# A two-sided recurrence on one core: half products and steps move only the 32 columns of a block that a level changes, and leave them packed in PSUM

## The reference, cut to what matters

```
def step(state, inp):
    r_t, w_t, k_t, v_t, kk_t, a_t = inp
    sa = jnp.einsum('bhvk,bhk->bhv', state, -kk_t)
    state = (state * w_t[:, :, None, :] + sa[..., None] * (kk_t * a_t)[:, :, None, :]
             + v_t[..., None] * k_t[:, :, None, :])
    return state, jnp.einsum('bhvk,bhk->bhv', state, r_t)
```

## Time and profile before

| | |
|---|---|
| median of 3 runs | 2564.86 us (2564.17 to 2568.09) |
| the profiled execution's own time | 2562.55 us |
| its span, first to last instruction | 2560.8 us |
| mean granted clock of PE | 0.994 of 2.4 GHz |
| PE, PEld, DVE, ACT, POOL busy | 2453.5, 2112.5, 1086.6, 475.1, 178.8 us |
| first and last half product (L3688) | 2061.2 and 2306.9 us |
| L3688, L3701 records | 1280; 1280 and 1024 |
| L3504, L3978 | 80 each |

### The profile page before, as it was taken

How to read it: one execution, slowest core, us unless ns; L and a number is a source line. 1 busy time by engine, 2 the same in 40 slices (tenths; PEclk the granted TensorE clock), 3 DMA queues, 4 the chain that set the end, 5 groups by cost and what they waited for, 6 DMA issues and landing times. The chain is left out here.

```text
span 2560.8 us, 80261 instructions
## 1 busy us (share of the span) xinstructions
PE 2453.5 (96%) x36137; PEld 2112.5 (82%) x36137; DVE 1086.6 (42%) x2659; ACT 475.1 (19%) x1059; POOL 178.8 (7%) x225
## 2 busy tenths in 40 slices
PE   7999999999999999999999999999999989989998
PEld 7898878789889989999999898777758767777775
DVE  4682554477321010110101102446764378866666
ACT  2111000211132323210000001410010445542000
POOL 0100000010022322210000000000000001110000
PEclk9999999999989999999999999999999999999999
DMA  7444553554589999999999999326564000020453
GB/s 234 154 148 139 175 164 131 171 179 149 202 306 407 408 407 408 407 408 407 407 407 407 407 406 329 116 90 200 197 209 161 3 7 8 7 71 26 166 177 117
DMA packets 289906, 571.11 MB, mean 223 GB/s; under 512 B 18190, under 2 KB 180244, under 8 KB 289764
## 3 DMA queue, kind: packets, MB, share of 16 engines
q1 hardware_dynamic: 289764, 569.10, 60.9%
HBM read 567.98 MB, written 5.28 MB: 224 GB/s over the span
## 5 line engine op out<-in xcount | busy, mean ns | idle before, releaser
L2669 PE MATMUL ps<-xg,ring 128*64 128x80 f32 x14336 | 508.6, 233 | 6.3 <-issue 4.7
L2669 PEld LDWEIGHTS ps<-xg,ring 128*64 128x64 f32 x14336 | 502.1, 138 | 10.9 <-issue 6.6
L2792 DVE TENSOR_TENSOR hidden<-acted,ps 128x320 f32<-128x320 f32 x64 | 28.5, 446 | 661.8 <-PE ps L2669 661.8
L2685 PE MATMUL ps<-hidden,expert_down 128*64 128x80 f32 x7168 | 257.3, 233 | 11.1 <-DMA expert_down<-in_moe_w_down_dram 5.3
L2685 PEld LDWEIGHTS ps<-hidden,expert_down 128*64 128x64 f32 x7168 | 251.4, 137 | 14.2 <-issue 9.8
L2734 ACT ACTIVATE ring<-second 128x1792 f32<-128x1792 f32 x60 | 101.9, 1699 | 213.4 <-PE ps L2669 139.8
L631 PE MATMUL ps<-xT,ring 128*128 128x256 f32 (+1 forms) x592 | 133.1, 384 | 3.1 <-DMA ring<-in_w_in_dram 3.1
L631 PEld LDWEIGHTS ps<-xT,ring 128*128 128x128 f32 (+1 forms) x592 | 107.0, 183 | 26.4 <-issue 3.5
L2726 POOL COPY ring<-second 128x1792 f32<-128x1792 f32 x60 | 100.9, 1681 | 309.4 <-PE ps L2669 181.1
L631 PE MATMUL ps<-ring,xT 128*128 128x256 f32 (+1 forms) x544 | 108.9, 361 | 2.2 <-PEq L1136 2.2
L631 PEld LDWEIGHTS ps<-ring,xT 128*128 128x128 f32 x544 | 96.0, 190 | 14.5 <-issue 3.0
(11 more groups left out here) (617 smaller groups left out, 3918.5 us busy)
## 6 DMA issues: line engine op xcount, KB each, us to landing
expert_down<-in_moe_w_down_dram SPq DMA_DIRECT2D x96, 1024.0 KB, 17.2
ring<-in_mlp_w_dram SPq DMA_DIRECT2D x64, 1024.0 KB, 5.3
ring<-in_moe_w_gate_dram SPq DMA_DIRECT2D x68, 896.0 KB, 16.0
ring<-in_moe_w_up_dram SPq DMA_DIRECT2D x68, 896.0 KB, 16.6
second<-in_moe_w_gate_dram SPq DMA_DIRECT2D x30, 1792.0 KB, 18.9
second<-in_moe_w_up_dram SPq DMA_DIRECT2D x30, 1792.0 KB, 18.8
ring<-in_w_xkv_dram SPq DMA_DIRECT2D x16, 1024.0 KB, 5.4
expert_down<-in_moe_w_down_dram SPq DMA_DIRECT2D x32, 512.0 KB, 16.5
```

What stands on the lines that cost most here:

```text
L2669: mm = pe.matmul(bank[b][o:o + HEAD, at, :], w[:, c, f * P + o:f * P + o + HEAD], xg[:, p * E_STEP + c, :], start=(p == 0 and c == 0 and a ...
L2685: mm = pe.matmul(yT[c // 4][o:o + HEAD, c % 4, :], w[:, j, c * P + o:c * P + o + HEAD], hidden[:, f, :], start=False, stop=False, skip_gro ...
L2792: dve.tensor_tensor(hidden[:, part, :], acted[:, part, :], src, ALU.mult).then_inc(hidden_ready, 1)
```

## The change

Half products and steps now move only the 32 columns that the level can change, and write them without gaps. `changing` picks them in the source. The half product writes 4 x 32 columns instead of 4 x 64, ACT copies those 128 columns and scatters them into Pb at their places, and the step writes its two kinds side by side into the last 128 columns of bank A(d) and the first 128 of B(d). DVE's predicated copy reads this packed stretch; it still moves 256 elements per partition (128 at level 5) into the same places of XX. Pb's other columns keep what is in them, which nothing reads into a result, so POOL fills both Pb with zeros at the start, and ACT waits for that once before the first pair. The weights keep 64 columns.

```
-        def both_kinds(d):
-
-            return ps[:, A(d):B(d) + 1, :].rearrange("p a b -> p (a b)")[:, 4 * HEAD:]
+        PART = HEAD // 2
+
+        def both_kinds(d, k):
+
+            packed = ps[:, A(d):B(d) + 1, :].rearrange("p a b -> p (a b)")[:, 12 * PART:20 * PART]
+            return packed.rearrange("p (r n m b) -> p r n m b", r=2, n=4, b=1 << k)
...
-            at = n * HEAD
+            at = n * PART
             if region(kind, d):
-                return ps[:, B(d), at:at + HEAD]
-            return ps[:, A(d), 4 * HEAD + at:4 * HEAD + at + HEAD]
+                return ps[:, B(d), at:at + PART]
+            return ps[:, A(d), 12 * PART + at:12 * PART + at + PART]
+
+        def changing(block, k, kind, d):
+
+            return block.rearrange("p (m z b) -> p m z b", z=2, b=1 << k)[:, :, region(kind, d), :]
...
+                pool.memset(Pb[0][:], 0.0)
+                pool.memset(Pb[1][:], 0.0).then_inc(self.cleared.sem, 1)
...
-                    act.activation(Pb[d][:].rearrange("p a b -> p (a b)"), ps[:, A(d), 0:4 * HEAD], ACT.Copy).then_inc(q["half_ready"].sem, 1)
+                    to = changing(Pb[d][:].rearrange("p a b -> p (a b)"), k, 0, d)
+                    act.activation(to, ps[:, A(d), 0:4 * PART].rearrange("p (m b) -> p m b", b=1 << k), ACT.Copy).then_inc(q["half_ready"].sem, 1)
...
+                act.wait_ge(self.cleared.sem, self.cleared.at(2))
...
-                            mm = pe.matmul(ps[other, A(d), n * HEAD:(n + 1) * HEAD], GM[d][h, n, 0, h], XX(i, d, 0, n)[h], start=True, stop=True)
+                            mm = pe.matmul(ps[other, A(d), n * PART:(n + 1) * PART], GM[d][h, n, 0, h], changing(XX(i, d, 0, n)[h], k, 0, d), start=True, stop=True)
...
-                                mm = pe.matmul(made(d, kind, n)[on], p if kind else xt, xt if kind else p, start=True, stop=True)
+                                mm = pe.matmul(made(d, kind, n)[on], p if kind else xt, changing(xt if kind else p, k, kind, d), start=True, stop=True)
...
-                    x, fresh, places = moved(XXs[d][i % 2][:], k), moved(both_kinds(d), k), places_of(k)
+                    x, fresh, places = moved(XXs[d][i % 2][:], k), both_kinds(d, k), places_of(k)
```

## The result

The changed kernel takes 2582.05 us (median of 6 runs, 2576.72 to 2585.77), the kernel before 2564.86 beside it (five runs): a ratio of 1.0059, 95% interval 1.0046 to 1.0071. It is slower, by 15 us by the ratio and 17 by the medians, and lies outside the range of the forecast (2553 to 2568). The profiled execution took 2579.67 us, 17.1 more than that of before; its span is 2577.9, the mean granted clock 0.980 (0.994 before).

The account below looks back on a forecast made before the run. No engine is full; PE's in-order chain waits for ACT's copy in four of ten slots, with DVE's slack limiting gains. Shorter copies and ends save 0.67 us a pair, 8 x 0.67 = 5.3: 2564.86 - 5.3 = 2559.5 us, range 2553 to 2568.

Parts of the forecast that it names:

- rival 3: PE's clock falls at levels 4 and 5; one dip in each pair gives 2569.2 us, two in some more; chance 0.16.
- A dip as long as the one from 1352.3 to 1355.7: Price of one clock fall at levels 4 and 5: it holds 1.4 slowed slots and costs 1.2 us.
- Decides from five dips on: Number of clock dips at which their 1.2 us each outweighs the 5.3 us gain (5.3 / 1.2 = 4.4).
- The main case: Shorter copy and ends save 0.67 us a pair, 5.3 in all: 2559.5 us, own range 2557.5 to 2562; chance 0.58.
- The pace of half products and steps: PE's records: the 64-wide weights set about 56 ns per record, so halving the moving columns changes nothing.
- rival 1: Weights don't bind PE; half products and steps each lose 0.22 us, DVE caps the gain: 2555.3 us; chance 0.12.
- ACT's copy: Copy of half products, 256 to 128 elements, saves 0.11 us in each of four slots at levels 4 and 5.
- The ends: The last record of a PE group ends 28 ns sooner, 0 as lower bound; alone worth 8 x 0.23 = 1.8 us.
- DVE's fit of 0.04 us: Last level-5 copy: DVE can start at 2208.50, PE asks for it at 2208.54, so it just fits.
- the cap that the prediction named: DVE has about as much slack as the change can give PE, which limits every gain.
- DVE's lead: From the first level-4 copy DVE runs 0.28 us ahead: 0.14 from its waiting there, 0.14 from earlier work.
- The level-1 copy: DVE's level-1 copy stays at 0.72 us; if the source in PSUM slows it, 0.3 us shorter, 1.5 in all.

Follow-up runs that it names:

- e1: The changed kernel plus one unused 128-column matmul before each step of levels 4 and 5; 2560.79 us, ratio 0.9977 to the kernel before.
- e5: The changed kernel plus the unused 128-column matmul before each step at level 4 alone; 2573.88 us, ratio 1.0029.
- e3: The changed kernel with steps of 64 columns again, not packed; half products and ACT's copy stay cut; 2563.75 us, ratio 0.9995.
- e8: e3 plus the unused matmul before each step at level 4; 2566.74 us, ratio 1.0007.
- e2: The kernel before with only ACT's copy cut to the changed columns, and the fills of Pb; 2564.19 us, ratio 0.9995.
- e4: The changed kernel with half products and ACT's copy of 64 columns again, only the steps cut; 2569.79 us, ratio 1.0013.
- e12: The changed kernel plus the unused 128-column matmul before each step at level 5 alone; 2577.82 us, ratio 1.0051.
- e7: The changed kernel with the next stage's weight loads begun after the last pair's first chunk is solved; 2572.35 us, ratio 1.0022.
- e6: The changed kernel plus 16 unused matmuls before each level-4 step, weights 32 or 64 wide by direction, to measure the pace; 2575.5 us in a single execution.
- e9: The kernel before with the next stage's weight loads begun after the last pair's first chunk is solved; 2563.95 us, ratio 0.9988.
- e10: e1 with the next stage's weight loads begun after the last pair's first chunk is solved; 2558.39 us, ratio 0.9975.
- e11: e3 with the next stage's weight loads begun after the last pair's first chunk is solved; 2557.66 us, ratio 0.9968.

## Why the prediction was wrong

**The step that failed** is the clock. The sum kept PE at full speed through all eight pairs, so it put the price of falls at nothing, and rival 3, which had them, was given 0.16 with the words "moving work halves and doesn't fall to an eighth, and a pair's other stretches are unchanged". Measured were 61 us at 1.2 GHz, which cost 17.5 us (8.1 in four periods, 9.5 in the last) against a gain of 1.0 in the other two. The place was named rightly (levels 4 and 5), and e1 shows the cause in the first six pairs: filling just these four slots takes all falls away. What I lacked was a row between 64 and 8 columns; the earlier trace rows only showed that 2.42 of 3.40 us busy at 64 is enough, and I read busy time as what counts. The windows with 2.49 us show that it isn't the busy time of the records.

**The price of a fall.** "A dip as long as the one from 1352.3 to 1355.7" was put at 1.2 us, and rival 3 had one in each pair, in some two. Where one of 3.4 us occurred (e5) a pair took 1.0 to 1.1 us more (32.61 and 32.72 against 31.59), so that was about right. But most falls of after lasted 6.8 and 10.2 us, and a pair with one took 2.0 to 3.0 us more than 31.60. "Decides from five dips on" was so put too high: after had four in its six full periods, and lost 8.1 us by them, net of the gain.

**What no rival had** is the last pair, 9.5 of the 17.1 us. Before paid some 3 us there for the early loads and PE's issue. The sentence ahead of the prediction that transfers play no part holds for the other pairs (DMA share 0.03) and not for this one (0.35 and 120 GB/s before). After the same idle time comes no fall in before and e3, one of 3.4 us in e8 and one of 10.2 in e2, all four with steps of 64 columns, and one of 27.3 us in after, e4, e5 and e12, with steps of 32. The earlier trace rows showed "issue 1.8", and I left it out as a thing that stays the same. e7 parts it from the rest: 13.4 us of the last period go, the other falls stay. Why instruction issue stands still is open: it never did with late loads, and with early ones it did in all but e1. Nor is it parted what else makes the last pair fall more easily: it has neither `keep_on` nor a next pair's matmuls.

**The main case, in undisturbed pairs**, was right in mechanism and off in size.
- The pace of half products and steps: no change, as predicted, and e6 refutes rival 1.
- ACT's copy: 0.27 us predicted, 279 ns measured; the level-4 waits 0.38 instead of 0.49, where I had 0.35. By itself it is worth 0.35 us a pair (e2), where 4 x 0.11 = 0.44 was summed. The earlier trace rows have the reason: 0.35 is the whole idle time of DVE before its last level-5 copy, and in e2 it is gone.
- The ends: 0.12 us came with the cut half products (e3 over e2) and 0.03 to 0.06 with the cut steps (31.60 against e3's 31.63; e4), together some 0.15 to 0.18, against 0.23. That these are the ends of the last records is an inference; their ends are modelled.
- DVE's fit of 0.04 us didn't hold: its two level-5 copies now run back to back, and the pair gained 0.50, not 0.67. That is the cap that the prediction named. The term that was too large is DVE's lead from the first level-4 copy on (2204.02 before, 2210.02 after), put at 0.28, of which half was to come out of the 0.17 us of idle time before that copy. Counted from the start of the pair's period, PE's step did start 0.25 us earlier (21.59 instead of 21.84 us), but the 0.17 stayed, and the copy came 0.14 earlier (22.58 instead of 22.72); with the 0.35 at level 5 that makes 0.50, within the rounding. Why that idle time stays wasn't tried.
- The level-1 copy stayed at 0.73 us with a packed source, as assumed. The Trainium skill, "Vector Engine (DVE) Microarchitecture Reference", section 5.2, has runs of two stream at the full rate in SBUF; the measurement speaks against the reading that the source in PSUM was to blame. Whether the destination's runs or the mask's cost the time wasn't tried.
- With 8 x 0.50 = 4.0 us and no fall the kernel would have come to about 2561 us, within the likeliest case's own range; e3, with periods of 31.63, has runs at 2558.5 to 2559.1 but a median of 2563.75; its four slowest executions (2568.52 to 2574.14) have a mean clock of 0.987 to 0.989, its four fastest 0.992 to 0.994.

The Trainium skill, "TensorE: Matmul & The Clock Gate", Part 1, says that the clock follows how busy the array was recently. The trace agrees in direction (e1), but the trace's busy time is no measure of it: behind a stretch with 2.49 us of 3.40 the clock fell in after (at 2111.3) and stayed up in e11, and the 8-column records of the earlier trace rows, busy for 3.40 of 3.40 us, lost it too.

## What to carry to other kernels

Before taking moving columns out of small matmuls whose weights stay wider, see that something is gained (here the weights set the pace), and look at the granted clock of the thinnest stretch: the columns that "cost nothing" may be what keeps PE at full speed, and a matmul put in while it waits anyway can give the clock back. Judge such a change by the undisturbed periods and by the disturbed ones apart. And try a later start of the next stage's large loads when they fall into a chain of short matmuls; here it was worth 3.2 us before and 13.4 after in the last pair.

## What the runs showed of the hardware

- Cutting the moving operand from 64 to 32 columns at the same weights left the pace at 0.63 us for 16 records, with 16 columns some 56 ns per record against 29 with weights of 32 (e6).
- 32 columns a matmul in half products and steps led to 61 us at 1.2 GHz in 284 us; the same with steps at 64 led to none in the profiled run (e3), and one matmul of 128 columns in four slots of each pair to none (e1). With all matmuls at 64 and the short copy alone there was one of 10.2 us, in the last pair (e2).
- A fall lasted 3.4 to 27.3 us, in a chain that otherwise differed by 0.5 us a pair.
- PE stood on issue for 1.5 to 1.9 us in the last pair in eight of the ten kernels that started the loads early (e6 for 0.91 us, e1 not at all), and in none of the four that started them later (e7, e9, e10, e11).
